# Half of a modulation's weight tiles weighed on GpSimd instead of TensorE, beside the grouped attention

## What is computed

```python
def ada_terms(cond, w_mod, b_mod):
    m = jax.nn.silu(cond) @ w_mod + b_mod
    return jnp.split(m, 6, axis=-1)
...
    for layer in range(DEPTH_2):
        ...
        sh1, sc1, gt1, sh2, sc2, gt2 = ada_terms(c[:, None, :], w_mod[layer], b_mod[layer])
        a = modulate_2(rms_norm_2(h, g_mix_pre[layer]), sh1, sc1)
...
def attend(q, k, v):
    s = jnp.einsum("bqkgd,bskd->bkgqs", q, k, preferred_element_type=F32) * (B_HEAD_DIM ** -0.5)
    p = jax.nn.softmax(s, axis=-1).astype(v.dtype)
    return jnp.einsum("bkgqs,bskd->bqkgd", p, v)
```

## Time and profile before

| | |
|---|---|
| runs | 2544.47, 2547.41, 2549.81 us (median 2547.41) |
| profiled execution | span 2544.2 us; its whole time is not listed apart from the span |
| TensorE busy (matmul) | 2076.1 us, 82% |
| VectorE busy | 704.8 us, 28% |
| ScalarE busy | 340.7 us, 13% |
| GpSimd busy | 107.1 us, 4% |
| grouped attention on TensorE | 1775.5 to 1820 us |

### The profile page before, as it was taken

The page is one execution under the profiler, slowest core; times in us unless marked ns, Lnnn a source line. Parts: engine busy times, 40 slices in busy tenths (PEclk is TensorE's granted clock), DMA queues, the critical chain, the costliest instruction groups (busy, mean ns, idle before and its releaser), DMA issues. The chain is left out here.

```text
span 2544.2 us, 35242 instructions
## 1 busy us (share of the span) xinstructions
PE 2076.1 (82%) x15498; PEld 1218.0 (48%) x15498; DVE 704.8 (28%) x1196; ACT 340.7 (13%) x688; POOL 107.1 (4%) x123
## 2 busy tenths in 40 slices
PE   7999998556666665677888865589999999999999
PEld 2445754212222332333455432255686884767873
DVE  4474742001110110112232210046542420651000
ACT  3002320000100000011110100022432000231000
POOL 0001100000000000001011100000210000100000
PEclk9999999999999999999999999999999999999999
DMA  9677238999999999999999999963303983314450
GB/s 381 267 290 281 78 133 367 424 424 424 424 424 420 420 419 422 422 405 424 424 424 423 425 423 425 424 248 126 123 3 120 309 308 106 119 64 138 160 207 25
DMA packets 159050, 755.19 MB, mean 297 GB/s; under 512 B 12265, under 2 KB 75881, under 8 KB 102194
## 3 DMA queue, kind: packets, MB, share of 16 engines
q1 hardware_dynamic: 158898, 752.94, 74.1%
HBM read 751.85 MB, written 1.05 MB: 296 GB/s over the span
## 5 line engine op out<-in xcount | busy, mean ns | idle before, releaser
L1270 PE MATMUL psum<-ring,arena 128*32 128x320 f32 x4064 | 352.9, 463 | 273.0 <-DMA ring<-w_gate_dram 136.9
L1270 PEld LDWEIGHTS psum<-ring,arena 128*32 128x32 f32 x4064 | 112.0, 110 | 427.3 <-DMA ring<-w_up_dram 166.5
L714 PE MATMUL psum<-arena,ring 128*128 128x256 f32 x1408 | 304.5, 379 | 0.0
L1336 PE MATMUL psum<-ring,arena 128*32 128x512 f32 x1344 | 210.5, 610 | 101.9 <-DMA ring<-w_down_dram 101.9
L714 PEld LDWEIGHTS psum<-arena,ring 128*128 128x128 f32 x1408 | 267.6, 190 | 36.7 <-issue 0.8
L612 PE MATMUL psum<-ring,arena 128*128 128x512 f32 x480 | 212.1, 603 | 4.9 <-DVE arena L1856 2.6
L2487 DVE TENSOR_TENSOR arena<-arena,psum 128x320 f32<-128x320 f32 (+1 forms) x32 | 16.7, 521 | 552.2 <-PE psum L1270 546.5
L1336 PEld LDWEIGHTS psum<-ring,arena 128*32 128x32 f32 x1344 | 48.3, 111 | 240.1 <-DMA ring<-w_down_dram 162.1
L612 PEld LDWEIGHTS psum<-ring,arena 128*128 128x128 f32 x480 | 92.4, 194 | 122.1 <-issue 119.9
L745 PE MATMUL psum<-ring,arena 128*128 128x512 f32 x288 | 124.8, 596 | 0.0
L1794 DVE SCALAR_TENSOR_TENSOR ring<-ring,cols 128x2048 f32<-128x2048 f32 x42 | 98.8, 2352 | 81.7 <-DMA ring<-w_mod_dram 80.3
(11 more groups left out here) (390 smaller groups left out, 2180.2 us busy)
## 6 DMA issues: line engine op xcount, KB each, us to landing
ring<-w_gate_dram SPq DMA_DIRECT2D x127, 1376.0 KB, 18.1
ring<-w_up_dram SPq DMA_DIRECT2D x127, 1376.0 KB, 18.1
ring<-w_down_dram SPq DMA_DIRECT2D x112, 1536.0 KB, 19.9
ring<-w_mod_dram SPq DMA_DIRECT2D x72, 1024.0 KB, 7.5
ring<-w_ffn_in_dram SPq DMA_DIRECT2D x88, 512.0 KB, 6.2
ring<-w_ffn_out_dram SPq DMA_DIRECT2D x14, 1536.0 KB, 8.3
ring<-w_in_dram SPq DMA_DIRECT2D x16, 1024.0 KB, 7.5
ring<-hyb_w_dram SPq DMA_DIRECT2D x10, 1024.0 KB, 16.7
```

Source lines behind the costliest of these rows:

```text
L714: ins = nc.tensor.matmul(b[:, i * 256:(i + 1) * 256], ws[k // 4][:, k % 4, u, i * P:(i + 1) * P], R(XT + k * 256, 256), start=(k == 0), st ...
L1270: ins = nc.tensor.matmul(banks[u][c][32 * j:32 * j + 32, 0:GMAIN], R(XST + k * HALF + e * CAP, CAP), w3[:, 64 * c:64 * c + 64, QGROUP * j: ...
L1336: ins = nc.tensor.matmul(ybanks[half][32 * c:32 * c + 32, :], stationary, w, start=((half, c) not in begun), stop=(unit >= 36), skip_group ...
```

## The change

Of the eight tiles of the first third, the even ones (k = 0, 2, 4, 6) are weighed on GpSimd into `weighed_sum(2)`, the last 1024 columns of slots 4 and 5; the odd ones stay on TensorE, at the steps i = 2, 6, 10 and 14 of the attention. After the attention TensorE waits for GpSimd's last tile and adds the partition sum of the weighed ones into the same bank 5 with four `pick_0` matmuls. GpSimd starts when the key and value projection has been done. The even tiles' slots are freed by GpSimd's semaphore instead of TensorE's. The SyncE queue gets one wait more, ahead of the feed-forward's down weights.

```diff
-            def modulation_part(tag, p, k, bank, cname="c2"):
-                if k == 0:
+            def modulation_part(tag, p, k, bank, cname="c2", first=0, last=KT - 1):
+                if k == first:
...
-            def weighed_part(tag, p, k):
+            def weighed_part(tag, p, k, by=mod_weighed):
                 enlist((tag, p, k))
-                freed_by[(tag, p, k)] = (mod_weighed, tally.due(mod_weighed))
+                freed_by[(tag, p, k)] = (by, tally.due(by))
...
             def beside_heads2(i):
-                if i % 2 == 0:
-                    modulation_part("mod2_1", 0, i // 2, 5)
+                if i % 4 == 0:
+                    weighed_part("mod2_1", 0, i // 2, mod_weighed_by_pool)
+                elif i % 4 == 2:
+                    modulation_part("mod2_1", 0, i // 2, 5, first=1, last=None)

             attention("gq", 16, scores2, values2, beside_heads2)
+            pe.wait_ge(*freed_by[("mod2_1", 0, KT - 2)])
+            for j in range(4):
+                ins = nc.tensor.matmul(psum[32 * j:32 * j + 32, 5, :], const("pick_0"), weighed_quarter(2, j),
+                                       start=False, stop=True, skip_group_check=True)
+                if j == 3:
+                    ins.then_inc(bank_filled[bank_of(("mod2_1", 0))], 1)
...
+            def weigh_modulation(tag, k):
+                key = (tag, 0, k)
+                w = slot(slot_of(key))[:, 0:2048].rearrange("p (s n) -> p s n", s=2)
+                c = col("c2")[:, k * 32:k * 32 + 1]
+                g.wait_ge(slot_loaded[slot_of(key)], count_of[key])
+                if k == 0:
+                    ins = g.tensor_scalar(weighed_sum(2), w, c, None, ALU.mult)
+                else:
+                    g.tensor_scalar(w, w, c, None, ALU.mult).then_inc(pool_done, 1)
+                    g.wait_ge(pool_done, tally.gave(pool_done))
+                    ins = g.tensor_tensor(weighed_sum(2), weighed_sum(2), w, ALU.add)
+                ins.then_inc(mod_weighed_by_pool, 1)
+                g.wait_ge(mod_weighed_by_pool, tally.gave(mod_weighed_by_pool))
...
+            g.wait_ge(bank_filled[bank_of(("bkv", 1))], nth(("bkv", 1)))
+            for k in range(0, KT, 2):
+                weigh_modulation("mod2_1", k)
             g.wait_ge(bank_drained[bank_of("gsums")], nth("gsums"))
             alternate(latent_delta(0), latent_delta(1))
...
-            s.wait_ge(bank_filled[bank_of(("mod2_1", 2))], nth(("mod2_1", 2)))
+            for p in (2, 0):
+                s.wait_ge(bank_filled[bank_of(("mod2_1", p))], nth(("mod2_1", p)))
             down_in("ffd0", T["w_ffn_out"][0])
```

More of the change, by code:

```diff
@@ L199, in program @@
         mod_weighed = semaphore("mod_weighed")
+        mod_weighed_by_pool = semaphore("mod_weighed_by_pool")
         post_gains_loaded = semaphore("post_gains_loaded")
@@ L495, in modulation_part @@
                 for j in range(4):
-                    ins = nc.tensor.matmul(psum[32 * j:32 * j + 32, bank, :], stat, w[:, j, :], start=(k == 0),
-                                           stop=(k == KT - 1), skip_group_check=True)
-                    if k == KT - 1 and j == 3:
+                    ins = nc.tensor.matmul(psum[32 * j:32 * j + 32, bank, :], stat, w[:, j, :], start=(k == first),
+                                           stop=(k == last), skip_group_check=True)
+                    if k == last and j == 3:
                         ins.then_inc(bank_filled[bank_of((tag, p))], 1)
@@ L502, in modulation_part @@
                     if j == 3:
-                        frees((tag, p, k), (tag, p) if k == KT - 1 else None)
-            def weighed_part(tag, p, k):
+                        frees((tag, p, k), (tag, p) if k == last else None)
+            def weighed_part(tag, p, k, by=mod_weighed):
                 enlist((tag, p, k))
-                freed_by[(tag, p, k)] = (mod_weighed, tally.due(mod_weighed))
+                freed_by[(tag, p, k)] = (by, tally.due(by))
             def modulation_sum(tag, p, bank, i):
```

## The result

Four runs of the change took 2575.21 us in the median (2572.03 to 2577.36), four of before 2547.53; the ratio is 1.0110, 95% interval 1.0099 to 1.0122. So it is slower by 25 to 31 us. The direction was forecast (+12.6 us), the size was not: 2575.2 lies above the range of 2550 to 2568.

The account below looks back on a forecast made before the run. VectorE's norms and rotation, key transposes and ScalarE were taken to set the pace until 1782.4, then TensorE. +17.4 (late attention) - 4.1 (tiles) + 1.1 (sum) - 1.8 (clock) = +12.6 us on 2547.4, 2560.0; range 2550 to 2568.

Parts of the forecast that it names:

- What is lost and where: VectorE's query and key norms and rotation take turns with GpSimd: keys 17.8 us late, attention starts 17.4 us late.
- Pairs of heads without and with a tile: In attention, pairs of heads take 3.7 and 4.8 us in turn, TensorE staying the bound.
- The price of GpSimd's operations: At 128x2048 a multiply costs 2.3 us (bounds 2.1 to 3.8), an add 3.8; seven operations 20.6 us.
- The hold of a multiply: VectorE's operations reading two SBUF tensors stand still until GpSimd's whole operation ends, one operation each in turn.
- One-input fast operations wait too: VectorE's L2604 and L2620 also wait for GpSimd: keys 17.8 us late; if not, 16.0, and the sum +10.8.
- TensorE's tiles and the clock: Over the heads: tiles 2, 4, 6 removed -4.1 us, partition sum added +1.1, clock -1.8.
- The clock's term: The slow stretch at 0.50 moves from the first heads to the first scores: 1.8 us won, bounds 0 and 2.0.
- tile 2's 1.94: The tile of k = 2 cost TensorE 1.94 us in the slow clock; its removal wins that much.
- Sum and slots: Four pick_0 matmuls behind the last head lose 1.1 us without waiting for GpSimd; moved loads and slot waits cost nothing.
- the engines hardly hinder each other: GpSimd's 20 us lie beside VectorE, whose two-input operations keep 0.69; only TensorE's -3.0 remains, 2544.4; chance 0.10.
- VectorE keeps its turn: GpSimd gets in only where VectorE reads PSUM or waits; keys 12.4 us late, sum +7.2, 2554.6; chance 0.10.
- The third, a dearer multiply: GpSimd's multiply costs the two-input price, 3.8 us; keys 24.4 us late, sum +19.2, 2566.6; chance 0.13.

Follow-up runs that it names:

- e6: e1_after_decay with GpSimd's multiplies and adds replaced by price probes at 128x2048; one run: constant multiply 5.37 us, copy 1.89, spread-column product 3.60.
- e9_multiply_wide: The change at its early place, with only GpSimd's multiply rewritten as a product with the spread column; 2568.2 us, ratio 1.0090 to before.
- e3: The change with each of GpSimd's seven operations replaced by a memset of the same 128x2048 output; ratio 1.0012 to before.
- e4: The change with each of GpSimd's seven operations cut into four of 128x512; 2557.44 us, ratio 1.0039 to before.
- e1_after_decay: The change, but GpSimd starts only when VectorE has finished the decays of the latent gates, beside the heads; 2546.44 us, ratio 0.9994 to before.
- e2: The change with GpSimd's seven operations each on only 8 of every 1024 columns, order and waits kept; ratio 1.0005 to before.

## Why the prediction was right in kind and wrong in size

- **What is lost and where**: right. The loss is VectorE's, in the norms and rotation of the queries and keys; the engines take turns of one operation. The chain keys, transposes, ScalarE's copies, scores carried it whole: keys 27.6 us late, scores 27.4. The forecast had 17.8 and 17.4. Pairs of heads without and with a tile took 3.77 and 4.76 us in turn, as forecast.
- **The price of GpSimd's operations** is the step that failed first. "It reads one tensor, so it is nearest to the copy: 2.3" was wrong, and so was the upper bound: I had said 2.1 to 3.8, and the multiply took 5.45. The constant in e6 costs the same, so the operation is dear as such: a one-input multiply (5.4) and a one-input copy (1.89) do not share a price on GpSimd. "On that line 2048 take 3.8" for the add was wrong too, 4.5: the rows behind it had a second operand that repeats itself in the program, as the spread column of e6 does. Products in e6 with such an operand, or of one tensor with itself, took 3.60; whether the operand or the add makes the difference e6 leaves open. Together 4 x 5.45 + 3 x 4.5 = 35.3 us instead of 20.6. The Trainium skill, GPSIMD Engine Reference, section "3.1 Elementwise — side-by-side cycle accounting", has a `tensor_tensor` add of 2048 at 4497 ns; the trace agrees (4.49 to 4.55 where it waited for nothing).
- **The hold of a multiply**: the forecast let every hold last to the end of GpSimd's operation. With the true prices that would have made the keys some 33 us late, by my estimate: seven turns, each 0.33 us shorter for VectorE than GpSimd's operation, as they are in e9_multiply_wide (27.9 us of GpSimd, 25.6 late), so 35.3 - 2.3. The 27.6 measured are fewer because a multiply holds two-input operations off for only 3.5 of its 5.45 us. What the prediction took from the Trainium skill, SBUF — State Buffer, section "Who interferes with whom", that the two exclude each other for the whole instruction, these rows bear out for the adds and not for the multiplies; the measurement decides.
- **One-input fast operations wait too**: chosen, with the other value kept as a bound; shown by L2613 in the change and in e3. The reason given, that it moves faster and so must use more of something, was not tested by itself, and e4 shows that how long they wait differs by GpSimd's size.
- **TensorE's tiles and the clock**: -4.1 + 1.1 - 1.8 = -4.8 was forecast for the heads, from the first transposes at 1782.36 to the gate sums. Measured: 35.58 us instead of 37.52, -1.9. The clock's term of -1.8 is the second step that failed. A slow stretch did lie over the first scores, as forecast (L1431 at 1806.50, 3.79 us; 1.99 at full clock in e1_after_decay). But it was not the only one, as the granted clock by stretch shows (columns as in the earlier trace rows). In the change:

```profile
1806.50:1810.20 3.70, 3.70 (x8) 1.24 (x8) 0.53 (x3) 2.65 (x4) 0.00 (x0) 0.50 0.00 0
1810.50:1813.50 3.00, 1.06 (x10) 0.17 (x3) 2.02 (x3) 2.25 (x4) 0.00 (x0) 1.00 0.39 82
1814.00:1820.50 6.50, 6.36 (x25) 4.74 (x25) 3.26 (x5) 2.11 (x6) 0.00 (x0) 0.50 0.66 260
```

  In e9_multiply_wide:

```profile
1809.00:1812.00 3.00, 3.00 (x10) 1.38 (x10) 1.08 (x2) 0.59 (x2) 0.00 (x0) 0.50 0.99 385
```

  A second stretch at 0.50 came over the first heads, about 6.8 us long, as long as the one of before (some 6.8 too; the 5.7 of the earlier trace rows were the window read). So nothing of the 1.8 came, and tile 2's 1.94 was worth only 1.07, since other work slid into the slow stretch in its place. e9 and e3 had both stretches as well, but the second lasted only about 3.4 us, and the heads took 34.38 and 34.39 us, -3.1. So tiles and clock together bring 1.9 to 3.1 us, by how long the slow stretch over the heads lasts.
- **Sum and slots**: the sum cost 1.07 and waited for nothing; GpSimd's last add ended at 1798.7. The other moves cost nothing, as e1 and e2 show.
- **Sum of the terms**: +27.4 - 1.9 = +25.5 in the stretch, against +12.6; the medians differ by 27.7, the interval's lower end is 25.2.
- **Rivals**: "the engines hardly hinder each other" fell: VectorE's two-input operations took 4.09 and 4.87 us instead of 0.69. So did "VectorE keeps its turn", by the strict alternation in e9. The third, a dearer multiply, was on the right side but priced at 3.8.

## What to carry to other kernels

Work given to an idle GpSimd cost nothing beside VectorE's maxima and copies from PSUM, and a one-input reduction in SBUF was not held either. Beside two-input or fast one-input VectorE operations in SBUF, even of 16 columns, each of them costs up to a whole GpSimd operation; so look at what VectorE does in the window first, start GpSimd by a wait on VectorE's last such operation, and cut its operations small if they must overlap. Measure GpSimd's operation at its own size: at 2048 columns a copy, a product and a multiply by a scalar took 1.89, 3.60 and 5.44 us. Even rightly placed, the tiles gave 1.8 to 2.8 us of 2547, which the whole time does not resolve.

## What was not expected of the hardware

- GpSimd's `tensor_scalar` on 128x2048 float32 takes 5.4 us, by constant or column, while a product with the column spread to a tensor takes 3.60 and a copy 1.89.
- That `tensor_scalar` holds VectorE's two-input operations off for its first 3.5 us only, and the fast one-input ones for nearly all of it; a memset holds off the latter alone. With 512 columns instead of 2048 a fast one-input operation was done 0.85 us before GpSimd's was.
- VectorE operations of 16 columns, 0.17 us alone, took up to 5.31 us.
- The granted clock fell to 0.50 (1.2 GHz) twice in the change, in e9 and in e3: over the first scores, and again over the first heads after 3 to 4 us at 1.00. Before and e1 had only the second. Ahead of the scores TensorE had waited 8.47, 17.27 and 1.04 us in the change, 17.77, 6.00 and 1.04 in e9, but only 1.82 and 1.22 in e3. What sets how often and how long it falls was not tried.
